# Dense gate and up of slices 1 to 6 by Strassen's seven half products, weight sums by adding DMAs in DRAM, weights in 1 MB blocks

## What is computed

```python
D_MODEL = 1024; SEQ = 256; D_FF = 3584
def swiglu(h, w_gate, w_up, w_down):
    return (jax.nn.silu(h @ w_gate) * (h @ w_up)) @ w_down
hn = rms_norm(h, ffn_norm[0])
h = h + swiglu(hn, dense_w_gate[0], dense_w_up[0], dense_w_down[0])
```

## Time and profile before

| | |
|---|---|
| median of 3 runs | 1490.58 us |
| span of the profiled execution | 1489.1 us |
| TensorE busy | 1477.0 us, 99% |
| VectorE, ScalarE, GpSimd busy | 1189.9, 947.9, 116.2 us |
| mean granted TensorE clock | 0.998 |
| TensorE's share of the chain that ended last | 96% |
| DMA moved | 445.60 MB |

### The profile page before, as it was taken

One profiled execution on the slowest core, in us unless ns is written; L12 is line 12 of the kernel. 1 busy time (PEld: TensorE's weight loads), 2 busy tenths in 40 slices (PEclk: granted clock), 3 DMA queues, 4 the chain that ended last, 5 costly groups with the idle time before them and its releaser, 6 DMA issues.

```text
span 1489.1 us, 20171 instructions
## 1 busy us (share of the span) xinstructions
PE 1477.0 (99%) x7900; PEld 1234.6 (83%) x7900; DVE 1189.9 (80%) x1056; ACT 947.9 (64%) x852; POOL 116.2 (8%) x77
## 2 busy tenths in 40 slices
PE   9999999999999999999999999999999999999998
PEld 7999988888887788888888888888888888888886
DVE  5977775444478699889889889898898988988985
ACT  4554544434465676777677777677777677767773
POOL 0470110000013000000000000000000000000000
PEclk9999999999999999999999999999999999999999
DMA  6331885555414299999999999999999999999990
GB/s 227 114 115 58 307 320 181 173 209 183 169 58 156 99 396 393 396 383 393 397 382 394 393 369 386 381 371 381 383 380 372 389 380 363 391 383 359 395 362 30
DMA packets 186696, 445.60 MB, mean 299 GB/s; under 512 B 5399, under 2 KB 5680, under 8 KB 186635
## 3 DMA queue, kind: packets, MB, share of 16 engines
q1 hardware_dynamic: 182208, 430.12, 77.7%
q0 software_dynamic: 3936, 14.20, 3.3%
q10 hardware_dynamic: 490, 0.42, 0.1%
HBM read 437.89 MB, written 7.89 MB: 299 GB/s over the span
## 4 chain that ended last, share of the span: by engine, by line
PE 96%; DVE 2%; DMA 1%; ACT 0%; POOL 0%; issue 0%; SPq 0%; DVEq 0%; ACTq 0%
PE bank L1482 14%; PE bank L1484 14%; PE bank L1483 14%; PE bank L1467 7%; PE bank L1469 7%; PE bank L1468 7%; PE bank L698 4%; PE bank L1145 3%; PE bank L1144 3%; PE bank L1143 3%; PE bank L785 2%; PE bank L789 2%; PE bank L790 2%; PE bank L791 2%; PE bank L1132 1%; PE bank L1130 1%
## 5 line engine op out<-in xcount | busy, mean ns | idle before, releaser
L2625 DVE TENSOR_TENSOR ring_r<-ring,buf_r 128x2048 fp32r<-128x2048 f32 x336 | 751.2, 2284 | 28.0 <-ACT buf_r L1926 28.0
L1926 ACT ACTIVATE buf_r<-ring 128x2048 fp32r<-128x2048 f32 x336 | 629.4, 1914 | 52.5 <-PE bank L1469 43.3
L1482 PE MATMUL bank<-ring_r,buf_r 128*128 128x512 f32 x896 | 354.5, 396 | 0.3 <-DVE buf_r L2745 0.3
L1484 PE MATMUL bank<-buf_r,buf_r 128*128 128x512 f32 x896 | 349.6, 390 | 0.0
L1483 PE MATMUL bank<-buf_r,buf_r 128*128 128x512 f32 x896 | 349.0, 389 | 0.0
L1484 PEld LDWEIGHTS bank<-buf_r,buf_r 128*128 128x128 f32 x896 | 168.0, 188 | 36.0
L1482 PEld LDWEIGHTS bank<-ring_r,buf_r 128*128 128x128 f32 x896 | 168.4, 188 | 33.6 <-DVE buf_r L2745 0.4
L1483 PEld LDWEIGHTS bank<-buf_r,buf_r 128*128 128x128 f32 x896 | 168.5, 188 | 33.4
L1467 PE MATMUL bank<-ring_r,buf_r 128*128 128x512 f32 x440 | 172.8, 393 | 0.1
L1469 PE MATMUL bank<-buf_r,buf_r 128*128 128x512 f32 x440 | 171.5, 390 | 0.0
L1468 PE MATMUL bank<-buf_r,buf_r 128*128 128x512 f32 x440 | 171.2, 389 | 0.0
(11 more groups left out here) (378 smaller groups left out, 1867.1 us busy)
## 6 DMA issues: line engine op xcount, KB each, us to landing
ring<-in_moe_w_gate SPq DMA_DIRECT2D x56, 2048.0 KB, 10.0
ring<-in_moe_w_up SPq DMA_DIRECT2D x56, 2048.0 KB, 10.4
ring<-in_moe_w_down SPq DMA_DIRECT2D x56, 2048.0 KB, 10.4
ring<-in_a_w_in SPq DMA_DIRECT2D x8, 2048.0 KB, 8.5
ring<-in_dense_w_gate SPq DMA_DIRECT2D x7, 2048.0 KB, 7.8
ring<-in_dense_w_up SPq DMA_DIRECT2D x7, 2048.0 KB, 7.9
ring<-in_dense_w_down SPq DMA_DIRECT2D x7, 2048.0 KB, 8.0
ring<-in_a_w_out SPq DMA_DIRECT2D x2, 2048.0 KB, 10.9
```

The lines of the kernel that those rows point to most:

```text
L1482: pe.matmul(o, xh, low[:, c], start=k == 0, stop=False)
L1484: ins = pe.matmul(o, xh, high[:, c], start=False, stop=k == KT - 1)
L1926: act.activation(HB[m % NHB], half_words(m, U_MOE), ACT.Copy).then_inc(m_wh, 1)
L2625: dve.tensor_tensor(half_low(m, U_MOE), half_words(m, U_MOE), HB[m % NHB], ALU.subtract).then_inc(m_wl, 1)
```

## The change

Slices 1 to 6 are taken in three pairs (p = 1, 2, 3). Gate of a pair is a product of (256 x 1024) by (1024 x 1024); up of the pair is another. Each is a *quad* (0 to 5), made by Strassen's scheme of 7 products of (128 x 512) by (512 x 512) in place of 8. A product is 4 x 3 = 12 matmuls of 128x512 on a weight block of 1 MB. Three of the seven blocks are quarters of the weights, four are sums of quarters. The four sums of a quad are made in DRAM (`weight_sums`): first 4 plain copies, then 2 + 1 + 1 adding DMAs (`accum_op=ALU.add`), each of 1 MB. The steps `sums_first`, `sums_second`, `sums_third`, `sums_fourth` do this for both quads of a pair, each waiting for the step before it (`sums_done`), and stand in POOL's queue between its other work. SyncE's queue loads 60 blocks of 1 MB in a ring of 12; one that is a sum waits for all 16 DMAs of its pair.

The mixed rows (four sums of quarters of the normed rows) are made once by VectorE and split. The outputs share three PSUM banks: ScalarE copies out the first and fifth product, VectorE adds and subtracts pieces (`sixth_part`, `last_piece`, `side_pieces`), POOL adds one piece for each quad (`both_parts`) and multiplies three of the four tiles of a pair by Silu of the gate (`quad_hidden`).

```diff
+            def sums_first(p):
+                j = 2 * p - 1
+                if p > 1:
+                    pool.wait_ge(sums_done, 16 * SUMS * (p - 1))
+                for qd in (2 * p - 2, 2 * p - 1):
+                    kind = quad_kind(qd)
+                    for r, src in ((0, quarter(kind, j, 0)), (2, quarter(kind, j + 1, 0)), (1, quarter(kind, j, 0)),
+                                   (3, quarter(kind, j, 1))):
+                        pool.dma_start(sums(qd, r), src).then_inc(sums_done, 16)
+            def sums_second(p):
+                pool.wait_ge(sums_done, 16 * (SUMS * (p - 1) + 8))
+...
+                        pool.dma_start(sums(qd, r), src, accum_op=ALU.add, max_dma_last_dim=2048).then_inc(sums_done, 16)
+            def sums_third(p):
+                pool.wait_ge(sums_done, 16 * (SUMS * (p - 1) + 12))
+                for qd in (2 * p - 2, 2 * p - 1):
+                    pool.dma_start(sums(qd, 1), sums(qd, 2), accum_op=ALU.add, max_dma_last_dim=2048).then_inc(sums_done, 16)
+            def sums_fourth(p):
+                pool.wait_ge(sums_done, 16 * (SUMS * (p - 1) + 14))
+...
+            pool.wait_ge(proj_mm, 2)
+            sums_first(1)
...
             for t in range(TT):
                 power(sm(264 + t * HEADS, HEADS))
+                if t == 0:
+                    sums_first(2)
+            sums_second(2)
             power(sm(192, 1))
...
             power(sm(193, 1))
+            sums_third(2)
+            sums_fourth(2)
...
+            for qd in range(QUADS):
+                both_parts(qd)
+                if qd == 0:
+                    sums_first(3)
+                if qd == 1:
+                    quad_hidden(1)
+                    sums_second(3)
+                    sums_third(3)
+                    sums_fourth(3)
+                elif qd % 2 == 1:
+                    quad_hidden(quad_pair(qd))
...
+            def quad_products(qd):
+                product(m, A_BANK, rows_of(0, 0), start=True)
+                product(m + 1, B_BANK, mixed(1), start=True)
+                product(m + 2, C_BANK, mixed(0), start=True)
+                pe.wait_ge(first_out, 2 * qd + 1)
+                product(m + 3, A_BANK, rows_of(1, 0))
+                pe.wait_ge(part_v, 4 * qd + 1)
+                product(m + 4, B_BANK, mixed(2))
+                pe.wait_ge(first_out, 2 * qd + 2)
+                product(m + 5, C_BANK, mixed(3))
+                pe.wait_ge(part_v, 4 * qd + 2)
+                product(m + 6, B_BANK, rows_of(1, 1))
+            def last_piece(qd):
+                dve.wait_ge(quad_p, pool_part(qd))
+                dve.wait_ge(d_used, quad_at(qd) + 5)
+                dve.scalar_tensor_tensor(out=o, in0=bk[B_BANK][:, :], scalar=-1.0, in1=o, op0=ALU.mult, op1=ALU.subtract
+                                         ).then_inc(part_v, 1)
```

More of the change, by code:

```diff
@@ L72, in slot_of, with uses_before @@
     return (n % FRONT if n < U_OUT else 5 * (n - U_OUT)) if n < U_FF else RING[(n - U_FF) % SLOTS]
+def uses_before(s):
+    return sum(slot_of(n) == s for n in range(U_KV))
 def uses(n):
-    return sum(slot_of(m) == slot_of(n) for m in range(n + 1))
+    s = slot_of(n)
+    blocks = sum(block_place(m)[0] == s for m in range(NB)) if n >= U_KV else 0
+    return sum(slot_of(m) == s for m in range(n + 1)) + blocks
 def fill_bank(kind, n):
@@ L392, in static_units @@
             u += [("c", cols(a_w_out[0], n)) for n in range(2)]
-            w = {"gate": dense_w_gate[0], "up": dense_w_up[0], "down": dense_w_down[0]}
-            u += [("r", rows(w[k], j)) if k == "down" else ("c", cols(w[k], j)) for k, j in ffn_sequence()]
             u += [("c", cols(kv_w, 0))]
@@ L622, in _ @@
                     level_mask(lv, g)
+                if lv == 3:
+                    sums_second(1)
                 if lv == 4:
@@ new lines, in _, with both_parts @@
+            pool.wait_ge(d_used, 4)
+            pool.dma_start(RBW[N_BUCKETS:N_BUCKETS + 1, :], c_main[0:1, one:one + SW_HEADS]).then_inc(rb_in, 16)
+            pool.dma_start(RBW[0:N_BUCKETS, :], rel_bias).then_inc(rb_in, 16)
+            pool.dma_start(RBT, c_table.rearrange("p (a c) -> p a c", c=P)).then_inc(rb_in, 16)
+            pool.dma_start(rows_dram.ap()[S:S + P, :], c_zero).then_inc(rows_out, 16)
+            def both_parts(qd):
+                out = (QPR if qd % 2 else QSG)[:, 1, 1, :].rearrange("p (k q) -> p k q", q=P)
+                pool.wait_ge(first_out, 2 * qd + 2)
+                pool.tensor_tensor(out, out, FIRSTP, ALU.add).then_inc(quad_p, 1)
@@ new lines, in down, with product @@
+                return ins
+            def product(m, bank, of, start=False):
+                pe.wait_ge(d_wl, m + 1)
+                low, high = block_low(m), block_high(m)
+                for k in range(4):
+                    c = slice(k * FS, (k + 1) * FS)
+                    ah, al = of(k)
+                    pe.matmul(bk[bank][:, :], ah, low[:, c], start=start and k == 0, stop=False, skip_group_check=not start)
+                    pe.matmul(bk[bank][:, :], al, high[:, c], start=False, stop=False, skip_group_check=not start)
+                    ins = pe.matmul(bk[bank][:, :], ah, high[:, c], start=False, stop=k == 3, skip_group_check=not start)
+                ins.then_inc(d_used, 1)
@@ new lines, in down_blocks @@
+            def down_blocks(j):
+                for m in (down_at(j), down_at(j) + 1):
+                    pe.wait_ge(d_wl, m + 1)
+                    if m % 2 == down_at(j) % 2:
+                        pe.wait_ge(ht_ready, 2 * j + 2)
+                    for t in range(TT):
+                        ins = down(m, t)
+                    ins.then_inc(d_used, 1)
+                    hidden_turns(m)
+            for qd in range(QUADS):
+                quad_products(qd)
+                p = quad_pair(qd)
+                if qd % 2 == 0:
+                    down_blocks(max(0, 2 * p - 3))
+                elif p > 1:
+                    down_blocks(2 * p - 2)
@@ new lines, in mixed_rows @@
+            def mixed_rows():
+                t0, t1 = slice(0, P), slice(P, S)
+                sums = [SRAW[:, i, :].rearrange("p (k q) -> p k q", q=P) for i in range(4)]
+                dve.wait_ge(hn_a, 4)
+                dve.wait_ge(wo_mm, 4)
+                then(dve.tensor_tensor(sums[0], HT[:, 4:8, t1], HT[:, 0:4, t1], ALU.subtract))
+                dve.tensor_tensor(sums[2], HT[:, 0:4, t0], HT[:, 0:4, t1], ALU.subtract)
+                then(dve.scalar_tensor_tensor(out=sums[1], in0=sums[0], scalar=-1.0, in1=HT[:, 0:4, t0], op0=ALU.mult,
+                                              op1=ALU.subtract))
+                dve.scalar_tensor_tensor(out=sums[3], in0=HT[:, 4:8, t0], scalar=-1.0, in1=sums[1], op0=ALU.mult,
+                                         op1=ALU.subtract).then_inc(hn_v, 1)
```

448 lines of the change are left out of this document (303 added, 145 removed).

## The result

The changed kernel takes 1624.1 us (median of four runs, 1622.3 to 1625.8), the kernel before 1490.6 on the same chip: a ratio of 1.090, with an interval of 1.088 to 1.091. The forecast was 1554, in a range of 1500 to 1605. The direction was right; the time is 70 us above the forecast and 19 above the range.

A forecast was written before the change was run, and what follows sets the result against it. The prediction took TensorE, 99% busy, to bound the kernel. Waits of 4 + 10 + 9 + 6 + 48 + 3 = 80 us less 16.3 gave +64, 1554 us, in a range of 1500 to 1605.

The forecast's parts named there:

- What it removes: Gate and up of slices 1 to 6: 72 fewer matmuls by 0.2268 us, -16.3 us, all on TensorE.
- The price of a sum: DRAM sums: an add 5.2 us for 1 MB, a copy 2.7, plus a fixed 6 us a step.
- Place 1: Unit 3's load, beside pair 1's eight copies, comes 7.7 us later; TensorE waits 0 to 8 us, taken as 4.
- Place 2: Level-5 masks, behind pair 1's third step waiting for its second: late by 7 to 14 us, taken as 10.
- Place 3: Pair 2's second step ahead of the power, its copies beside w_out's loads: 0 to 20 us, taken as 9.
- Place 4: Quad 0's 7th product waits for its piece behind pair 2's later steps: 0 to 12 us, taken as 6.
- Place 5: Quad 2's 7th product waits for its piece behind pair 3's later steps: 17.6 to 66 us, taken as 48.
- Place 6: VectorE's splits, pieces and low parts against TensorE's products in the dense stage: 0 to 8 us, taken as 3.
- GpSimd's piece: A piece on GpSimd could cost 0.5 us more by contention with VectorE; changes a term by less than its range.
- Loads alone are not a bound: Dense stage: loads and pair 3's sums take 157 us of the engines against 167 us, just enough.
- engines choke: Rival: DRAM to DRAM copies and adds cost more, step two 60 us: +110 to +150, 1600 to 1640 us; chance 0.11.
- never late: Rival: pair 3's sums are in before `both_parts(2)`, TensorE keeps the -16 us: 1474 to 1484 us; chance 0.07.

The follow-up runs named there:

- run 4: The changed kernel with each adding DMA made a plain copy of the same quarter (weight sums left out): 1572.9 us, ratio 1.056.
- run 7: The changed kernel, all computed, with later sum steps moved on GpSimd's queue behind the small work they held up: 1629.1 us, ratio 1.093.
- run 1: The changed kernel without its 48 sum DMAs, blocks that held sums loaded from plain quarters of the weights: 1501.9 us, ratio 1.008.
- run 6: The changed kernel without sum DMAs, with evictions of hidden-row tiles moved one or two blocks earlier on ScalarE and VectorE: 1478.3 us, ratio 0.992.
- run of two pairs: The changed kernel with GpSimd's steps and the evictions moved, sums made for pairs 2 and 3 only, pair 1 from plain quarters: 1574.7 us.
- runs 7 and 8: Run 8 is the changed kernel with GpSimd's steps moved as in run 7 and the evictions moved too, all computed: 1610.5 us, ratio 1.081.

## Why the prediction was wrong, step by step

- *What it removes*, -16.3 us: right. Without sums and stalls TensorE is busy for 1461.5 us, 15.5 less than before.
- *The price of a sum*, 5.2 us a MB against a copy's 2.7: right, 5.5 and 2.6. The steps were a bit longer: up to 39.8 us for four adds (27 to 34 used, 40 the bound), and 22.9 for two (up to 20 used). The earlier trace rows were misread in one point, without effect on the sum: the two queues had 143 and 327 packets there, not about as many.
- *Place 1*, unit 3's split, 0 to 8, taken as 4: 11.4, outside its bounds. Unit 3's split by ScalarE starts at 66.6 us, not 50.8: 15.8 late, where the prediction had its load 7.7 late. SyncE's queue had less than the 161 GB/s of the earlier trace rows beside DRAM to DRAM copies: 2.31 MB from 42 to 66 us, 96 GB/s.
- *Place 2*, the level-5 masks, 10: 7.2. Right in place and size.
- *Place 3*, w_out and the rows' norm, 9: 12.6 in four pieces. Right, though by another way: the last of pair 2's eight copies was issued 31.2 us after the seventh. The same gap is in the run of the kernel before with sums, and not in run 4; its cause is open.
- *Place 4*, quad 0's piece, 6: 13.6. The steps ahead of it were issued some 30 us later than reckoned (second at 222 for 192), by place 3.
- *Place 5*, quad 2's piece, 48: 36.2. Right in mechanism, within its bounds. But it is not a cost that can be taken away by moving the piece: run 7 moved it, with the steps behind it, and 35.7 us stood at the next place. Places 1 to 5 add up to 81 us where 77 were forecast, and that is luck: 12 too many here hide most of the 19 too few at places 1, 3 and 4.
- *Place 6*, VectorE and the turns, 0 to 8, taken as 3: **this term failed.** 38.4 us: 18.8 are the form's own (run 1), the rest blocks that come late, with ScalarE in its order behind them (its splits at 328, 344 and 362 us waited 11.6, 11.9 and 7.5 us for their loads). The prediction compared VectorE's work with TensorE's, and the turns as 4.9 against 2.7 us "now and then". It did not follow the one thing that decides: whose eviction stands behind which split. In pair 3 the split of block 56 waits until block 54 is used (`high_place` shifts for the last four), and the eviction of a turn stands behind it on ScalarE. Moving the evictions gave 23.6 us back (run 6).
- *GpSimd's piece*, 1.4 us, up to 0.5 more beside VectorE: `both_parts` took 2.0 to 2.8 us (six, median 2.3), the shortest in run 4 1.3. The masks of 5.02 and 7.02 us which were compared are two different instructions, and the second takes 7.02 in the changed kernel too. No run here tells what makes the piece longer.
- *The clock*, not in the sum: **29.0 us, the second failure.** The prediction put this term at nothing, with no reason given. In eleven stretches TensorE's 128x512 matmuls stand 0.43 us apart, not 0.23, mostly after idle time, so that such a stall is paid for twice; half of the work in these stretches is 25.7 us. The traces of before had no stall to show it, but a bound on it was to be kept, and was not.
- *Loads alone are not a bound*, 157 us of engines against 167: wrong too, and it hid the late blocks of place 6. It counted pair 3's sums and left out pair 2's, whose eight adds run from 222 to about 305 us in the same stage: 8 x 5.5 = 44 us more. With them it reads 201 against 167.

The sum by these: 11.4 + 7.2 + 12.6 + 13.6 + 36.2 + 38.4 = 119.4 us of waits where 80 were forecast, and 29 of clock. Either failure alone would have left the time in the range: without the clock's 29.0 it is 1595, with place 6 at its bound of 8 it is 1594. Together they put it at 1624. The rival *engines choke* had the right time (1600 to 1640) with the wrong reason: adds were not dearer than forecast, and a second step took up to 39.8 us, not 60; there were too many in too little time. The rival *never late* put its time at 1474 to 1484; as written, the change takes 1501.9 even with no sums at all, and only with the turns moved, too, 1478.3. Its condition, a fixed part of under 1 us a step, was reckoned wrong: with no fixed part at all the steps of place 5 take 10.7 + 5.3 + 1.5 + 2.1 = 19.6 us at the copy's price, and TensorE leaves 14.

No run computes everything and beats the kernel before. By the table it is not near: one pair alone can give 16.3 / 3 = 5.4 us, and the cheapest pair that was measured costs 20.5.

## What to carry to other kernels

Before a change moves work to an idle resource, count all of it against the time until its date, not only the part that ends last: here 44 us of a second pair's adds turned "just enough", 157 of 167 us, into 34 too many. Then look at the order of the queue that issues it: with the engines free, a step that stands behind something else is as late as one that waits for them (20 us in the run of two pairs). When products become shorter than the split and eviction behind them, write out, for each eviction, what stands ahead of it on its engine and what that waits for. And price a stall of TensorE at its idle time plus a few us at half clock behind it; here stalls of 120 us in all cost 26 to 29 us more than they were long.

## What the runs showed of the hardware

- After most idle stretches TensorE worked at a granted clock of 0.5: ten matmuls 0.426 us apart after the wait of 36.2 us, some 3.5 us of it after one of 5.0 (run 1, to 404 us), 7 after one of 7.2 (the changed kernel, 133 to 140 us), and in run 1 a window of 6 us at 0.50 behind a wait of 7.2. Not after all: behind the waits of 1.8 us in run 1 (342 us) and of 3.6 in the changed kernel (357 us) the clock was 1.00.

```profile
415.00:421.00 6.00, 5.80 (x16) 4.74 (x17) 2.94 (x3) 0.60 (x1) 0.00 (x0) 0.50 0.14 50
421.00:427.00 6.00, 6.00 (x30) 4.92 (x29) 0.69 (x1) 2.42 (x5) 0.00 (x0) 0.99 0.00 0
```

- A DMA that adds from DRAM to DRAM moved 2 KB a packet and kept the engines busy for 5.5 us a MB; a copy of the same quarters moved 3.9 KB a packet and cost 2.6. In run 4 the copies that stand for the adds carry the adds' argument `max_dma_last_dim=2048` and still moved 3.9 KB a packet, at 2.6 us a MB (its second step of pair 3, 321 to 343 us, below): the shorter packets come with the adding. Whether they or the adding itself make the price, no run here separates.

```profile
q0 software_dynamic: 1088, 4.19, 49.9%
```

- Beside eight such copies a weight load of 2 MB was ready to be split 15.8 us later than alone.
- The eighth DMA in a row on GpSimd's queue was issued 31.2 us after the seventh, with full engines and nothing else to wait for:

```profile
180.03 1.86 POOL L760 DMA_DIRECT2D weight_sums<-in_dense_w_up  x3
...
213.11 0.63 POOL L760 DMA_DIRECT2D weight_sums<-in_dense_w_up  x1 [31.23 <-issue]
```

The first eight, at 29.8 us, went out within 5.1 us, and in run 4, where the adds before it are copies, this same burst went out in 5.0 us (from 167.4). In runs 7 and 8 the gap was 26 us. So it isn't a matter of the eighth DMA, nor of full engines alone; the run of the kernel before with sums has it too (30.6 us). What sets it is open.
